# Layer boundaries of a transformer kernel: stage inputs turned and scaled by a product with a diagonal

## The chip, the cores and the metric

The kernel runs on one core of one Trainium2 chip. The metric is the device time in microseconds of one execution. TensorE is PE in the rows (its weight loads PEld), VectorE is DVE, ScalarE is ACT, GpSimd is POOL, and SP is the engine that issues the loads of weights.

## The reference, cut to what matters

256 tokens of 1024 channels pass through latent attention with a convolutional FFN, differential attention with such an FFN, and a hybrid layer (gated delta net, rotary attention, two gates). Each of these five parts has the form below. `g_pre` has one gain per channel, the root one value per token.

```python
def rms_norm(x, g):
    xf = x.astype(jnp.float32)
    y = xf * lax.rsqrt(jnp.mean(xf * xf, -1, keepdims=True) + EPS)
    return (y * g.astype(jnp.float32)).astype(x.dtype)
...
    x = x + rms_norm(part(rms_norm(x, g_pre)), g_post)
```

## The kernel before, in words

The tokens stand on the partitions in `hid` (two token tiles t = 0, 1 of 128 tokens by 1024 channels, f32). The projections need the input turned: `xh` and `xl` hold it with the channels on the partitions, eight blocks b of 128 channels by 256 tokens, as a high part (rounded to the fast f32 format) and the low rest. Every weight chunk is split in the same way (`split_high` L361 on ScalarE, `split_low` L372 on DVE or GpSimd), and `mm3` (L409) makes a product of three fast ones. `project_t` (L421) runs 24 such matmuls over the eight blocks; its argument `arriving` makes the first projection of a stage wait for the low parts of the input as they come.

Between two parts lies a boundary, numbered n for the part that ends (n = 0 latent attention, 1 first FFN, 2 differential attention, 3 second FFN, 4 the end). Every engine has its program written out by hand, and semaphores tie them; an engine's order is the order of the calls.

- The end of the part, `post_*` (L641 to L702). ScalarE squares the accumulators and sums them (`post_square`), DVE multiplies them with the post gain (`post_gained`), adds up the mean, GpSimd raises it to -0.5 (`post_pool`, L674), DVE adds the result to `hid` (`post_add`, L669). `post_dve` (L690) sets DVE's order over tiles and halves (half = 512 channels).
- The input of the next part. ScalarE squares `hid` (`pre_square`, L549), DVE makes the mean (`pre_mean`, L559), GpSimd the root (`pre_pool`, L632). DVE then multiplies each tile and half with root and gain (`pre_norm`, L567, the gain `pre_gain` broadcast over all partitions by DMA), TensorE turns the result (`pre_pe`, L527: first seven filler products L525, then sixteen transpositions L535, then one filler), ScalarE copies the high part (`pre_split_act`, L555) and DVE subtracts (`pre_split_dve`, L627). This serves three boundaries: before the first FFN, before the second FFN, before the delta net. `boundary_pool` (L743) and `start_pool` (L765) load the gains from GpSimd's queue.
- The boundary before differential attention ("the raw boundary", RAW = 2) differs: `raw_pe` (L572) turns `hid` itself, without the root, both token tiles of a block side by side in one bank (`raw_turned`, L584), ScalarE and DVE split with the gain as a per-channel scale (`raw_split_act` L591, `raw_split_dve` L599), and the root enters later through `factor_cols_dve` (L610).

The filler products (`spin`, L522) compute nothing that is used. Behind the splits ScalarE and DVE have weight splits in their queues, then the first convolution of the FFN (L1208, L1252). The delta net begins with the product for its gates (`gates_project_pe`, L1691).

Of the kernel before, what the change touches and what calls it, by code (L numbers as in the profile page):

```python
# [23 lines left out]
P = 128  # L24
TOK = 256
# [84 lines left out]
for _n, _w in (("q_gain", MLA_QB), ("kv_gain", MLA_KVB), ("sub_gain", 1),  # L110
               ("gdn_gain", 1), ("down_gain", KB), ("power", 8), ("conv", HEADS * 12), ("ffn_conv", 2 * FFN_STEPS * 16),
               ("slope", HEADS), ("dt", 2 * HEADS), ("a_log", 2 * HEADS), ("lam", 256), ("diff_gain", KB)):
    _vec(_n, _w)
# [65 lines left out]
def lay_out(a):  # L179
# [34 lines left out]
    pre = np.stack([ng[0, 0], ng[0, 2], ng[1, 0], ng[1, 2], f["pre_norm_w_2"][0]])  # L214
    out["post_gain"] = np.ascontiguousarray(np.broadcast_to(post[:, None], (5, P, D)))
    out["pre_gain"] = np.ascontiguousarray(np.broadcast_to(pre[[1, 3, 4], None], (3, P, D)))
# [53 lines left out]
def build(nc, dram, y_out):  # L270
# [150 lines left out]
    def project_t(pe, out, k, width=P, offset=0, x=None, blocks=KB, arriving=None):  # L421
# [71 lines left out]
    n_ = sems("n", "hid sq mean root hn turned xh xl gain")  # L493
# [94 lines left out]
    def raw_split_act(act, half):  # L588
        act.wait_ge(n_["turned"], 4 * RAW + 2 + half + 1)
        for b in range(4 * half, 4 * half + 4):  # L590
            ins = act.activation(xh[:, b, :], raw_turned(b), ACT.Copy, scale=vcol("diff_gain", b, 1))  # L591
            if b % 2:
                ins.then_inc(n_["xh"], 1)

    def raw_split_dve(dve):
        for b in range(KB):
            if b % 2 == 0:
                dve.wait_ge(n_["xh"], 4 * RAW + b // 2 + 1)
            ins = dve.scalar_tensor_tensor(xl[:, b, :], raw_turned(b), vcol("diff_gain", b, 1), xh[:, b, :], ALU.mult,  # L599
                                           ALU.subtract)  # L600
            if b % 2:
                ins.then_inc(n_["xl"], 1)
# [9 lines left out]
    def factor_pe(pe):  # L612
        pe.wait_ge(n_["hn"], 4 * (RAW - 1) + 2)
# [4 lines left out]
    def factor_dve(dve):  # L618
        dve.wait_ge(n_["hn"], 4 * (RAW - 1) + 3)
        dve.tensor_copy(factor, acc[:, 3, 0:TOK]).then_inc(n_["hn"], 1)  # L620
        dve.wait_ge(n_["hn"], 4 * (RAW - 1) + 4)

    def pre_split_dve(dve, n):
        for half in range(2):
            for t in range(NT):
                dve.wait_ge(n_["xh"], 4 * n + 2 * t + half + 1)
                dve.tensor_tensor(x_part(xl, t, half), turned(t, half), x_part(xh, t, half),  # L627
                                  ALU.subtract).then_inc(n_["xl"], 1)
# [61 lines left out]
    def post_dve(dve, n, p, k):  # L690
# [5 lines left out]
        post_mean(dve, n, 1)  # L696
        post_gained(dve, n, 1, 0, p, k)
        post_add(dve, n, 0, 1)
# [9 lines left out]
    def pre_act_split(act, n):  # L708
        for t in range(NT):
            pre_split_act(act, n, t)  # L710

    def pre_dve(dve, n):
        pre_norm(dve, n, 0, 0)
        pre_mean(dve, n, 1)
        pre_norm(dve, n, 0, 1)
        for half in range(2):
            pre_norm(dve, n, 1, half)
# [6 lines left out]
    def boundary_raw_act(act, n, p, k):  # L724
        post_act(act, n, p, k)
        pre_square(act, RAW, 0)
        for half in range(2):
            raw_split_act(act, half)
        pre_square(act, RAW, 1)

    def boundary_raw_dve(dve, n, p, k):
        post_early_dve(dve, n, p, k)
        raw_split_dve(dve)
# [9 lines left out]
    def boundary_pool(pool, n):  # L743
# [21 lines left out]
    def start_pool(pool):  # L765
# [5 lines left out]
        pool.dma_start(pre_gain[:], dram["pre_gain"][0]).then_inc(n_["gain"], 16)  # L771
# [919 lines left out]
    def gates_project_pe(pe):  # L1691
        chunk_ready(pe, ph["gates"], 4, 0)
        for b in range(KB):
            if b % 4 == 0:
                pe.wait_ge(n_["xl"], 4 * 4 + 2 + b // 2)
            last = mm3(pe, W[2][0:16, 0:TOK], wslot(4, b * 16, (b + 1) * 16), (xh[:, b, :], xl[:, b, :]), b == 0, b == KB - 1)
# [1477 lines left out]
```

## Time and profile before

| | us |
|---|---|
| median of three runs | 1056.98 |
| lowest and highest | 1056.97, 1057.31 |
| the profiled execution, its own time | 1056.94 |
| its span in the profile | 1055.1 |
| TensorE busy in the span | 1026.9 (97%) |
| DVE, ScalarE, GpSimd busy | 667.6, 557.1, 418.1 |

The rows come from the one profiled execution. Times in them are microseconds from the start of the span; 1.8 us of the execution's time lie around it. The idle time of an engine that is not on the chain of waits costs nothing.

### The profile page before, as it was taken

How to read it: one execution, taken by the hardware profiler on the slowest of the kernel's cores; microseconds unless marked ns; L12 is line 12 of the kernel's file. 1: busy time of each engine (PE TensorE's matmuls, PEld its weight loads, DVE VectorE, ACT ScalarE, POOL GpSimd, SP SyncE). 2: the span in 40 equal slices, each digit the busy share in tenths (PEclk: the TensorE clock that was granted, in tenths of full speed). 3: DMA queues.
4: the chain of work that ended last, by engine and by line, in shares of the span. 5: the costliest groups of instructions: out<-in, count | busy, mean ns of one | idle time of the engine just before them, and what ended most of it. 6: DMA issues, size and time to landing. Idle time of an engine off the chain costs nothing.

```text
span 1055.1 us, 21644 instructions
## 1 busy us (share of the span) xinstructions
PE 1026.9 (97%) x8138; PEld 941.0 (89%) x8138; DVE 667.6 (63%) x1094; ACT 557.1 (53%) x1014; POOL 418.1 (40%) x283
## 2 busy tenths in 40 slices
PE   9999999999999999999999999999999999999997
PEld 7788699999978888699999987899999999999996
DVE  4555867767767766777676766766676555554445
ACT  5655665555564654665555556644543455554442
POOL 1000243334333443433343363865653375533331
PEclk9999999999999999999999999999999999999999
DMA  9334456566434443365655624333213245446551
GB/s 354 102 120 140 159 182 206 188 201 191 151 138 160 156 135 128 124 210 184 201 191 167 205 77 160 104 119 120 81 62 121 81 140 157 151 135 215 195 181 42
DMA packets 46284, 161.82 MB, mean 153 GB/s; under 512 B 5264, under 2 KB 6544, under 8 KB 46096
## 3 DMA queue, kind: packets, MB, share of 16 engines
q1 hardware_dynamic: 45072, 156.79, 44.7%
q0 software_dynamic: 1152, 4.19, 1.2%
q8 instruction: 42, 0.69, 0.3%
q14 instruction: 18, 0.15, 0.0%
HBM read 159.91 MB, written 1.05 MB: 153 GB/s over the span
## 4 chain that ended last, share of the span: by engine, by line
PE 89%; DVE 5%; ACT 2%; POOL 2%; issue 1%; DMA 0%; DVEq 0%; SPq 0%; ACTq 0%
PE work L411 13%; PE work L413 13%; PE work L412 13%; PE work L1849 9%; PE acc L411 6%; PE acc L412 6%; PE acc L413 6%; PE work L2567 4%; PE work L2579 3%; PE acc L2579 2%; PE acc L2096 1%; PE acc L2110 1%; PE acc L2112 1%; PE acc L1941 1%; PE work L1387 1%
## 5 line engine op out<-in xcount | busy, mean ns | idle before, releaser
L380 POOL TENSOR_TENSOR low<-raw,high 128x1024 fp32r<-128x1024 f32 x110 | 269.0, 2449 | 276.5 <-ACT high L367 274.0
L380 DVE TENSOR_TENSOR low<-raw,high 128x1024 fp32r<-128x1024 f32 (+1 forms) x185 | 271.0, 1473 | 147.9 <-ACT high L367 147.8
L367 ACT ACTIVATE high<-raw 128x1024 fp32r<-128x1024 f32 (+2 forms) x295 | 298.6, 1026 | 36.6 <-DMA raw<-in_w_out 23.7
L411 PE MATMUL work<-xh,high 128*128 128x256 f32 (+1 forms) x1032 | 290.0, 281 | 2.1 <-DVE v_sb L1534 1.7
L412 PE MATMUL work<-xl,high 128*128 128x256 f32 (+1 forms) x1032 | 287.9, 279 | 0.0
L413 PE MATMUL work<-xh,low 128*128 128x256 f32 (+1 forms) x1032 | 287.8, 279 | 0.0
L411 PEld LDWEIGHTS work<-xh,high 128*128 128x128 f32 (+1 forms) x1032 | 193.2, 187 | 9.0 <-issue 5.6
L412 PEld LDWEIGHTS work<-xl,high 128*128 128x128 f32 (+1 forms) x1032 | 193.3, 187 | 1.7
L413 PEld LDWEIGHTS work<-xh,low 128*128 128x128 f32 (+1 forms) x1032 | 193.3, 187 | 0.2
L1290 POOL TENSOR_TENSOR h<-gelu,cv 128x256 f32<-128x256 f32 x44 | 49.7, 1130 | 194.3 <-ACT gelu L1214 87.6
L1849 PE MATMUL work<-xh,high 128*128 128x256 f32 x256 | 76.7, 300 | 0.0
L1849 PE MATMUL work<-xl,high 128*128 128x256 f32 x256 | 71.6, 280 | 0.0
L1849 PE MATMUL work<-xh,low 128*128 128x256 f32 x256 | 71.4, 279 | 0.0
L412 PE MATMUL acc<-low,hh 128*128 128x512 f32 x164 | 64.3, 392 | 0.0
L411 PE MATMUL acc<-high,hh 128*128 128x512 f32 x164 | 64.2, 391 | 0.0
L413 PE MATMUL acc<-high,hl 128*128 128x512 f32 x164 | 63.8, 389 | 0.0
L1220 ACT ACTIVATE hh<-h 128x256 fp32r<-128x256 f32 x42 | 17.5, 418 | 86.7 <-POOL h L1290 85.7
L1849 PEld LDWEIGHTS work<-xh,high 128*128 128x128 f32 x256 | 48.1, 188 | 2.5
L1849 PEld LDWEIGHTS work<-xl,high 128*128 128x128 f32 x256 | 48.2, 188 | 0.0
L1849 PEld LDWEIGHTS work<-xh,low 128*128 128x128 f32 x256 | 48.1, 188 | 0.0
L1208 ACT ACTIVATE cv<-work,vec 128x256 f32<-128x256 f32 x44 | 24.8, 564 | 40.0 <-PE work L413 40.0
L1293 POOL TENSOR_TENSOR hl<-h,hh 128x256 fp32r<-128x256 f32 x42 | 31.9, 760 | 25.6 <-ACT hh L1220 25.6
(402 smaller groups left out, 2172.5 us busy)
## 6 DMA issues: line engine op xcount, KB each, us to landing
raw<-in_w_ffn SPq DMA_DIRECT2D x130, 512.0 KB, 4.3
raw<-in_w_out SPq DMA_DIRECT2D x39, 512.0 KB, 4.3
raw<-in_w_att SPq DMA_DIRECT2D x32, 512.0 KB, 3.9
raw<-in_w_diff SPq DMA_DIRECT2D x31, 512.0 KB, 3.9
raw<-in_w_gdn SPq DMA_DIRECT2D x24, 512.0 KB, 4.4
raw<-in_w_mla SPq DMA_DIRECT2D x8, 512.0 KB, 3.7
raw<-in_w_gdnz SPq DMA_DIRECT2D x8, 512.0 KB, 4.0
raw<-in_w_mla SPq DMA_DIRECT2D x8, 384.0 KB, 3.3
```

The lines of the kernel that those rows point to most:

```text
L367: act.activation(high[k][:, 0:w], raw[k][:, 0:w], ACT.Copy).then_inc(high_done[k], 1)
L380: eng.tensor_tensor(low[k][:, 0:w], raw[k][:, 0:w], high[k][:, 0:w], ALU.subtract).then_inc(low_done[k], 1)
L411: pe.matmul(out, lhs[0], rhs[0], start=start, stop=False)
L412: pe.matmul(out, lhs[0], rhs[1], start=False, stop=False)
L413: return pe.matmul(out, lhs[1], rhs[0], start=False, stop=stop)
L1208: act.activation((cg, cv)[value][j][:], W[bank][:, 0:TOK], ACT.Identity, scale=ffn_taps(layer, i, j, value, 1, 0), bias=ffn_taps(layer, i, ...
L1220: act.activation(hidden_of(layer, j, i)[0][:], h32[j][:], ACT.Copy).then_inc(f[j]["hh"], 1)
L1290: pool.tensor_tensor(h32[j][:], gelu[j][:], cv[j][:], ALU.mult).then_inc(s["h32"], 1)
L1293: pool.tensor_tensor(low_part[:], h32[j][:], high_part[:], ALU.subtract).then_inc(s["hl"], 1)
L1849: last = pe.matmul(W[x][:, 0:TOK], l[slot][:, b * P:(b + 1) * P], r[:, b, :], start=(s == 0), stop=(s == 23))
L2567: last = pe.matmul(W[0][:, t * TOK:(t + 1) * TOK], x[:, b, t * P:(t + 1) * P], w[k][:, o:o + TOK], start=(b == 0 and term == 0), stop=(b = ...
L2579: last = pe.matmul(out, w[k][:, b * P:(b + 1) * P], x[:, b, :], start=(s == 0), stop=(s == 23))
```

## The change

At the three boundaries the input is turned by a product in full f32 instead of a transposition: the moving operand is no longer the identity but the identity with each token's root on its diagonal, so that the product turns `hid` and scales it at once. DVE makes that diagonal (128x128) in place of the norm of 128x1024 per tile. TensorE goes through the channels by halves and, within a half, through both token tiles, and puts a block's two tiles side by side. ScalarE and DVE split with the gain per channel as at the raw boundary, in blocks of 128x256, eight in place of four of 128x512. The gains of four boundaries stand in the vector table, and the three loads of broadcast gains are dropped. There is one filler fewer in front of the products and none behind. DVE's `post_add` of tile 0, half 1 moves ahead of `post_gained` of tile 1, half 0. The raw boundary keeps its operations and counts block by block. The gates' product goes to another bank. One wait of ScalarE for the constants moves ahead of the first boundary. The diff, cut to its core:

```diff
 def lay_out(a):
-    put("diff_gain", channels(ng[1, 0]))
+    put("pre_gain", np.concatenate([channels(x) for x in (ng[0, 2], ng[1, 0], ng[1, 2], f["pre_norm_w_2"][0])], 1))
...
-    out["pre_gain"] = np.ascontiguousarray(np.broadcast_to(pre[[1, 3, 4], None], (3, P, D)))
 def project_t(...):
-            if arriving == RAW and b % 2 == 0:
-                pe.wait_ge(n_["xl"], 4 * RAW + 1 + b // 2)
-            elif arriving is not None and b % 4 == 0:
-                pe.wait_ge(n_["xl"], 4 * arriving + 2 + b // 2)
+            if arriving is not None and b % 2 == 0:
+                pe.wait_ge(n_["xl"], split_seen(arriving) + b + 2)
...
+    def split_seen(n):
+        return 4 + KB * (n - 1)
+    HN_SEEN = {1: 0, 2: 2, 3: 6, 4: 8}
 def pre_pe(pe, n):
     pe.wait_ge(g["const"], 48)
-        spin(pe, W[3][:], 7)
-        for t in range(NT):
-            for half in range(2):
-                pe.wait_ge(n_["hn"], 4 * (n - 1) + 2 * t + half + 1)
-                for b in range(4):
-                    at = (4 * half + b) * P
-                    last = pe.transpose(work[:, 2 * t + half, b * P:(b + 1) * P], hn[:, t, at:at + P], ident)
+        spin(pe, W[3][:], 6)
+        for half in range(2):
+            for t in range(NT):
+                pe.wait_ge(n_["hn"], HN_SEEN[n] + t + 1)
+                for b in range(4 * half, 4 * half + 4):
+                    last = pe.matmul(raw_turned(b)[:, t * P:(t + 1) * P], hid[:, t, b * P:(b + 1) * P], diag[t],
+                                     start=True, stop=True)
                 last.then_inc(n_["turned"], 1)
-        spin(pe, acc[:, 3, :], 1)
-    def pre_split_act(act, n, t):
-        for half in range(2):
-            act.wait_ge(n_["turned"], 4 * n + 2 * t + half + 1)
-            act.activation(x_part(xh, t, half), turned(t, half), ACT.Copy).then_inc(n_["xh"], 1)
-    def pre_norm(dve, n, t, half):
-        dve.wait_ge(n_["root"], 2 * n + t + 1)
-        if t == 0 and half == 0:
-            dve.wait_ge(n_["gain"], 16 * (n if n < RAW else n - 1))
-        c = cols(half)
-        dve.scalar_tensor_tensor(hn[:, t, c], hid[:, t, c], stat[:, 8 + t:9 + t], pre_gain[:, c], ALU.mult,
-                                 ALU.mult).then_inc(n_["hn"], 1)
+    diag = [hn[:, t, 0:P] for t in range(NT)]
+    def pre_diag(dve, n, t):
+        dve.wait_ge(n_["root"], 2 * n + t + 1)
+        dve.tensor_scalar(diag[t], ident, stat[:, 8 + t:9 + t], None, ALU.mult).then_inc(n_["hn"], 1)
...
-    def raw_split_act(act, half):
-    def raw_split_dve(dve):
+    def turned_gain(n, b):
+        return vcol("pre_gain", KB * (n - 1) + b, 1)
+    def pre_split_act(act, n, half):
+        act.wait_ge(n_["turned"], 4 * n + (2 + half + 1 if n == RAW else 2 * half + 2))
         for b in range(4 * half, 4 * half + 4):
+            act.activation(xh[:, b, :], raw_turned(b), ACT.Copy, scale=turned_gain(n, b)).then_inc(n_["xh"], 1)
+    def pre_split_dve(dve, n):
         for b in range(KB):
             if b % 2 == 0:
+                dve.wait_ge(n_["xh"], split_seen(n) + b + 2)
+            dve.scalar_tensor_tensor(xl[:, b, :], raw_turned(b), turned_gain(n, b), xh[:, b, :], ALU.mult,
+                                     ALU.subtract).then_inc(n_["xl"], 1)
 def post_dve(dve, n, p, k):
         post_mean(dve, n, 1)
+        post_add(dve, n, 0, 1)
         post_gained(dve, n, 1, 0, p, k)
-        post_add(dve, n, 0, 1)
         post_add(dve, n, 1, 0)
 def pre_dve(dve, n):
-        pre_norm(dve, n, 0, 0)
+        pre_diag(dve, n, 0)
         pre_mean(dve, n, 1)
-        pre_norm(dve, n, 0, 1)
-        for half in range(2):
-            pre_norm(dve, n, 1, half)
+        pre_diag(dve, n, 1)
 def boundary_pool(pool, n):
-        if n in (0, RAW):
-            pool.wait_ge(n_["hn"], 4 * n + 4)
-            pool.dma_start(pre_gain[:], dram["pre_gain"][1 if n == 0 else 2]).then_inc(n_["gain"], 16)
 def start_pool(pool):
-        pool.dma_start(pre_gain[:], dram["pre_gain"][0]).then_inc(n_["gain"], 16)
 def gates_project_pe(pe):
-            if b % 4 == 0:
-                pe.wait_ge(n_["xl"], 4 * 4 + 2 + b // 2)
-            last = mm3(pe, W[2][0:16, 0:TOK], ...)
+            if b % 2 == 0:
+                pe.wait_ge(n_["xl"], split_seen(4) + b + 2)
+            last = mm3(pe, acc[0:16, 0, 0:TOK], ...)
```

## Rows read from the trace of the kernel before

**Rows 1.** Page, part 4, the chain of waits: share of the span by engine

```profile
PE 89%; DVE 5%; ACT 2%; POOL 2%; issue 1%; DMA 0%; DVEq 0%; SPq 0%; ACTq 0%
```

**Rows 2.** The chain in order of time, first boundary (start us, us, what)

```profile
119.23 1.00 POOL stat L632
...
122.38 0.86 PE acc L525 x2
```

**Rows 3.** Timeline from 118.9 us (start, us, engine, line, op, out<-in, count, idle before)

```profile
118.94 0.21 DVE L559 TENSOR_SCALAR mean<-stat 128x1 f32<-128x1 f32 x1
...
120.25 1.41 DVE L567 SCALAR_TENSOR_TENSOR hn<-hid,stat,pre_gain_sb 128x512 f32<-128x512 f32 x2 [0.44 <-POOL stat L632]
...
121.06 1.32 PE L535 MATMUL work<-const,hn 128*128 128x128 f32 x8 [0.54 <-DVE hn L567]
...
121.75 1.26 ACT L555 ACTIVATE xh<-work 128x512 fp32r<-128x512 f32 x2 [0.59 <-PE work L535]
...
122.38 1.29 DVE L627 TENSOR_TENSOR xl<-work,xh 128x512 fp32r<-128x512 f32 x2
...
123.22 0.35 PE L411 MATMUL work<-xh,high 128*128 128x256 f32 x1
...
126.10 0.28 PE L411 MATMUL work<-xh,high 128*128 128x256 f32 x1
```

**Rows 4.** Timeline, 112 to 118 us

```profile
112.81 6.17 PE L525 MATMUL work<-const 128*128 128x512 f32 x14
...
114.83 0.68 DVE L656 TENSOR_TENSOR hn<-acc,post_gain_sb 128x512 f32<-128x512 f32 x1
...
115.43 1.41 DVE L669 SCALAR_TENSOR_TENSOR hid<-hn,stat,hid 128x512 f32<-128x512 f32 x2
...
117.25 0.99 POOL L632 TENSOR_TENSOR stat<-mean,vec 128x1 f32<-128x1 f32 x1 [1.70 <-DVE mean L559]
...
117.86 0.63 ACT L549 ACTIVATE hn<-hid 128x512 f32<-128x512 f32 x1 [0.27 <-DVE hid L669]
```

**Rows 5.** Timeline, raw boundary, DVE

```profile
316.40 0.29 DVE L610 TENSOR_SCALAR hn<-const,stat 128x128 f32<-128x128 f32 x1 [0.47 <-POOL stat L632]
```

**Rows 6.** Timeline, raw boundary, from 310.9 us

```profile
310.94 3.03 ACT L591 ACTIVATE xh<-work,vec 128x256 fp32r<-128x256 f32 x8 [1.26 <-PE work L580]
...
311.06 0.55 POOL L632 TENSOR_TENSOR stat<-mean,vec 128x1 f32<-128x1 f32 x1 [1.72 <-DVE mean L559]
...
311.81 3.23 DVE L599 SCALAR_TENSOR_TENSOR xl<-work,vec,xh 128x256 fp32r<-128x256 f32 x8 [0.83 <-ACT xh L591]
...
312.83 0.35 PE L411 MATMUL work<-xh,high 128*128 128x256 f32 x1 [0.41 <-DVE xl L599]
...
315.12 0.36 PE L411 MATMUL work<-xh,high 128*128 128x256 f32 x1
...
315.90 0.28 PE L411 MATMUL work<-xh,high 128*128 128x256 f32 x1
```

**Rows 7.** The chain in order of time, delta net, products in f32

```profile
659.76 3.57 PE acc L1712 x32
```

**Rows 8.** The chain in order of time, raw boundary

```profile
310.94 0.85 ACT xh L591 x2
311.81 0.89 DVE xl L599 x2
```

**Rows 9.** Timeline, start of the first FFN, DVE

```profile
126.96 0.48 DVE L1252 SCALAR_TENSOR_TENSOR cg<-work,vec,cg 128x255 f32<-128x255 f32 x1 [0.42 <-ACT cg L1208]
```

**Rows 10.** Page, part 2 (GB/s by slice) and part 6 (DMA issues)

```profile
GB/s 354 102 120 140 159 182 206 188 201 191 151 138 160 156 135 128 124 210 184 201 191 167 205 77 160 104 119 120 81 62 121 81 140 157 151 135 215 195 181 42
...
pre_gain_sb<-in_pre_gain POOLq DMA_DIRECT2D x3, 512.0 KB, 4.9
```

**Rows 11.** List of waits, the longest for a DMA (us in total, times, longest)

```profile
ACT high L367 <- DMA raw<-in_w_out: 23.7, 6, 4.5
```

**Rows 12.** Busy time by stretch: PE, PEld, DVE, ACT, POOL, granted clock, DMA

```profile
118.00:123.00 5.00, 4.23 (x21) 2.10 (x19) 4.17 (x8) 2.97 (x7) 2.32 (x4) 1.00 0.29 93
```

More of the change, by code:

```diff
@@ L111 @@
                ("gdn_gain", 1), ("down_gain", KB), ("power", 8), ("conv", HEADS * 12), ("ffn_conv", 2 * FFN_STEPS * 16),
-               ("slope", HEADS), ("dt", 2 * HEADS), ("a_log", 2 * HEADS), ("lam", 256), ("diff_gain", KB)):
+               ("slope", HEADS), ("dt", 2 * HEADS), ("a_log", 2 * HEADS), ("lam", 256), ("pre_gain", 4 * KB)):
     _vec(_n, _w)
@@ L210, in lay_out @@
     put("power", np.full((P, 8), -0.5))
-    put("diff_gain", channels(ng[1, 0]))
+    put("pre_gain", np.concatenate([channels(x) for x in (ng[0, 2], ng[1, 0], ng[1, 2], f["pre_norm_w_2"][0])], 1))
     out["vec"] = v
     post = np.stack([ng[0, 1], ng[0, 3], ng[1, 1], ng[1, 3], f["post_norm_w_2"][0]])
-    pre = np.stack([ng[0, 0], ng[0, 2], ng[1, 0], ng[1, 2], f["pre_norm_w_2"][0]])
     out["post_gain"] = np.ascontiguousarray(np.broadcast_to(post[:, None], (5, P, D)))
-    out["pre_gain"] = np.ascontiguousarray(np.broadcast_to(pre[[1, 3, 4], None], (3, P, D)))
     def chunks(name, parts):
@@ L492, in build @@
     g = sems("g", "x second_x const")
-    n_ = sems("n", "hid sq mean root hn turned xh xl gain")
+    n_ = sems("n", "hid sq mean root hn turned xh xl")
     h = sems("h", "qkev s mx sm e p pt ptev vev pv oh ol rope roped turned turned_ev")
@@ L586, in raw_turned @@
         return work[:, b // 2, (b % 2) * TOK:(b % 2) * TOK + TOK]
-    def raw_split_act(act, half):
-        act.wait_ge(n_["turned"], 4 * RAW + 2 + half + 1)
+    def turned_gain(n, b):
+        return vcol("pre_gain", KB * (n - 1) + b, 1)
+    def pre_split_act(act, n, half):
+        act.wait_ge(n_["turned"], 4 * n + (2 + half + 1 if n == RAW else 2 * half + 2))
         for b in range(4 * half, 4 * half + 4):
-            ins = act.activation(xh[:, b, :], raw_turned(b), ACT.Copy, scale=vcol("diff_gain", b, 1))
-            if b % 2:
-                ins.then_inc(n_["xh"], 1)
-    def raw_split_dve(dve):
+            act.activation(xh[:, b, :], raw_turned(b), ACT.Copy, scale=turned_gain(n, b)).then_inc(n_["xh"], 1)
+    def pre_split_dve(dve, n):
         for b in range(KB):
             if b % 2 == 0:
[L598 to L602, printed above, removed]
+                dve.wait_ge(n_["xh"], split_seen(n) + b + 2)
+            dve.scalar_tensor_tensor(xl[:, b, :], raw_turned(b), turned_gain(n, b), xh[:, b, :], ALU.mult,
+                                     ALU.subtract).then_inc(n_["xl"], 1)
     factor_col = [hn[:, t, 0:P] for t in range(NT)]
@@ L612, in factor_pe @@
     def factor_pe(pe):
-        pe.wait_ge(n_["hn"], 4 * (RAW - 1) + 2)
+        pe.wait_ge(n_["hn"], HN_SEEN[RAW] + 2)
         for t in range(NT):
@@ L618, in factor_dve @@
     def factor_dve(dve):
-        dve.wait_ge(n_["hn"], 4 * (RAW - 1) + 3)
+        dve.wait_ge(n_["hn"], HN_SEEN[RAW] + 3)
         dve.tensor_copy(factor, acc[:, 3, 0:TOK]).then_inc(n_["hn"], 1)
-        dve.wait_ge(n_["hn"], 4 * (RAW - 1) + 4)
-    def pre_split_dve(dve, n):
-        for half in range(2):
[L625 to L628, printed above, removed]
+        dve.wait_ge(n_["hn"], HN_SEEN[RAW] + 4)
     def pre_pool(pool, n, t):
@@ L708, in pre_act_split @@
     def pre_act_split(act, n):
-        for t in range(NT):
-            pre_split_act(act, n, t)
+        for half in range(2):
+            pre_split_act(act, n, half)
     def pre_dve(dve, n):
-        pre_norm(dve, n, 0, 0)
+        pre_diag(dve, n, 0)
         pre_mean(dve, n, 1)
-        pre_norm(dve, n, 0, 1)
-        for half in range(2):
-            pre_norm(dve, n, 1, half)
+        pre_diag(dve, n, 1)
     def boundary_act(act, n, p, k):
@@ L726, in boundary_raw_act @@
         pre_square(act, RAW, 0)
-        for half in range(2):
-            raw_split_act(act, half)
+        pre_act_split(act, RAW)
         pre_square(act, RAW, 1)
@@ L732, in boundary_raw_dve @@
         post_early_dve(dve, n, p, k)
-        raw_split_dve(dve)
+        pre_split_dve(dve, RAW)
         diff_setup_dve(dve)
@@ L1693, in gates_project_pe @@
         for b in range(KB):
-            if b % 4 == 0:
-                pe.wait_ge(n_["xl"], 4 * 4 + 2 + b // 2)
-            last = mm3(pe, W[2][0:16, 0:TOK], wslot(4, b * 16, (b + 1) * 16), (xh[:, b, :], xl[:, b, :]), b == 0, b == KB - 1)
+            if b % 2 == 0:
+                pe.wait_ge(n_["xl"], split_seen(4) + b + 2)
+            last = mm3(pe, acc[0:16, 0, 0:TOK], wslot(4, b * 16, (b + 1) * 16), (xh[:, b, :], xl[:, b, :]), b == 0, b == KB - 1)
         last.then_inc(used[4], 1)
@@ L1717, in gates_take_act @@
         act.wait_ge(used[4], ph["gates"].base[4] + 1)
-        act.activation(gates_t, W[2][0:16, 0:TOK], ACT.Copy).then_inc(z_["act"], 1)
+        act.activation(gates_t, acc[0:16, 0, 0:TOK], ACT.Copy).then_inc(z_["act"], 1)
     def gates_beta_act(act):
@@ L3094, in _ @@
         mla_act(act)
+        act.wait_ge(g["const"], 48)
         boundary_act(act, 0, ph["mla"], 2)
@@ L3097, in _ @@
         split_high(act, ph["ffn0"], 4, 0)
-        act.wait_ge(g["const"], 48)
         ffn_act(act, 0)
```

## The prediction, made before the changed kernel was built or run

> **What bounds the kernel now.** I read the chain of waits on the page first: 89% of the end-setting chain is TensorE work [rows 1], so a change pays only where TensorE waits. The chain in order of time shows where that is, in this change's reach: at each of three layer boundaries (start of the first FFN, of the second, of the delta net) it leaves TensorE for the norms. At the first it goes through the second power on GpSimd, 1.00 us, and comes back to TensorE by the filler product L525 at 122.38 [rows 2]. The timeline shows that the filler hides a second path of equal length: the second low part L627 began at 122.38 and took 0.68 us (half the 1.29 for two, plus overlap), so it was there at 123.06; the projection began at 123.22 and its next one at 126.10 [rows 3]. The three boundaries repeat this to within 0.03 us, so I work out one. All are followed by stretches in which TensorE never waits, so what its projection gains or loses arrives at the end.
>
> **The change, part by part** (first boundary; before against after).
>
> Order of the adds. Before, gain (1,0) starts at 114.83 and the two adds at 115.43, 1.41 us for both: 0.75 each, 0.66 from start to start, so the second add starts at 116.09 [rows 4]. After, add (0,1) starts at 114.83, the gain at 115.49, ending 0.68 later at 116.17, and add (1,0) must wait for that: 116.21, taking 0.04 us for the handover. That add is 0.12 us later. But add (1,1) was held by a mean that waited for a square; that square now runs 0.6 us earlier, so mean and add follow at once: 116.87 and 117.00, add done 117.75. Before, it was done 0.03 us ahead of the square at 117.86 [rows 4]: 0.08 us won.
>
> Squares, mean and powers. ScalarE's last square starts 0.03 us after the add, at 117.78; its sum is read at 118.51. The first power took 0.99 us beside a DVE add with two operands in SBUF [rows 4]; the same in place, 117.16 to 118.15. The first diagonal then costs what L610 costs for the same form, 0.28 us [rows 5], and is ready at 118.46, where the norm of one half took 0.75. The mean of the second token tile no longer stands behind that norm: 118.55 instead of 118.94 [rows 3]. Its power starts at 118.83. Here is a choice: beside a norm it took 1.00 [rows 2]; at the raw boundary, with DVE idle, 0.55 [rows 6]. After the change DVE has nothing to do at that moment, so I take 0.55 and keep 0.99 for the range: 119.38. Second diagonal 119.41 to 119.69, against a norm that started at 120.25.
>
> Six fillers instead of seven: 12 instructions at 0.43 from 112.81 [rows 4] end near 118.1, before the first diagonal, so they delay nothing; seven would have ended at 119.0 and delayed the first products by half a microsecond, though not the second tile's.
>
> The products. A 128x128 product in full f32 is two instructions here, a transposition one. Thirty-two such instructions at L1712 took 3.57 us, 0.11 each [rows 7], so a product costs 0.22 and a group of four 0.89 us. First half of the channels: tile 0 runs at 118.5 to 119.4 in the wait; tile 1 starts at 119.75 (0.06 after the diagonal, as L535 after its norm [rows 3]) and its last result is there at 120.84. ScalarE may then split both tiles side by side: 120.88, against 121.75 for the corresponding block before [rows 3]. That is 0.87 us won.
>
> A rule could speak against this. The Trainium skill, "FP8 and Floating Point Precision", section TensorE Precision Notes, counts true FP32 as four passes through the array; read as four transpositions a product would cost 0.45, and the sum would come out near +8 us instead of about nothing. Rival C works that case out from rows.
>
> The evacuation. Before, one plain split of 128x512 (1.26 us for two) and one subtraction followed. After, the raw boundary is the pattern, same operations, same shapes, same buffers: ScalarE start 310.94, TensorE 312.83, so 1.89 us [rows 6], two splits 0.85 and two low parts 0.89 of it [rows 8]. TensorE would start at 120.88 + 1.89 = 122.77 instead of 123.22: 0.45 us earlier.
>
> What is late next. The low parts come at 0.39 us each (3.23 for eight, 0.89 for two [rows 6, 8]), TensorE eats a block in 0.35, so it stutters: at the raw boundary it started block 6 at 315.12 and the next projection at 315.90, 3.07 us after its start [rows 6]; before, here, the same stretch takes 2.88 [rows 3]. That gives back 0.19. And here, unlike there, the second half's sixteen instructions run after the first half's: their last starts at 122.35, is done at 122.62, and ScalarE's fifth split waits until 122.66 where its own pace (0.36 each) allowed 122.32. Sixth split done 123.51, fifth low part 123.54 instead of 123.33: 0.21 us more. Next projection: 122.77 + 3.07 + 0.21 = 126.05 against 126.10. **0.05 us per boundary**, 0.15 for three. With the second half's delay gone it would be 0.26; with the power at 0.99, a loss of 0.39.
>
> Behind it. ScalarE ends its splits at about 124.2 (before 123.0) and DVE at 125.2 (before 124.3), so the weight splits queued behind them are a microsecond late, and the first tap, which before started at 126.96 after a 0.42 us wait [rows 9], comes near 127.5. No product needs it before the second step, about 8 us on. Zero, at most 0.1 per FFN. At the delta net both engines wait for the gates' product anyway.
>
> Removed transfers. Three of 512 KB leave GpSimd's queue [rows 10], with about 0.5 us of issue each. Behind the first stands a power that waits for DVE long after, behind the second the first FFN's product that waits for a gelu, behind the third a weight split, which then starts a microsecond earlier for a product that TensorE reaches only after three projections (8 us). In the first slice 354 GB/s flow [rows 10], so the first is worth 1.5 us of transfer there; yet the longest wait for a transfer is of the last stage [rows 11], and none follows that load. Zero; 1.5 is its bound. The 24 more columns of the vector table, the earlier wait of ScalarE for constants long loaded, and the raw boundary's single-step counts: zero, since nothing in it moves.
>
> The end of the kernel. The last boundary has the new order too, and there add (1,0) feeds add (1,1) with no mean between: the 0.12 us stay. Loss 0.12.
>
> Sum: -0.15 + 0.12 = -0.03 us on the profiled execution's 1056.94, which is the median of 1056.98 to 0.04. **1057.0.** A measurement can tell about 0.2%, 2.1 us, from no change.
>
> **The rivals.**
> A. The gain comes whole (faster). If the transfer at the start did delay weights, 1.5 us return; if the second half doesn't hold up ScalarE, 3 x 0.26 more: -2.3 + 0.12 gives 1054.8. For it: transfers fill the first slice. Against: no wait on them behind that load. It needs both. 0.07.
> B. The power stays at 0.99 because its cost isn't the neighbour on DVE: 3 x 0.39 + 0.12 = +1.3, 1058.2. The two prices at the same line speak against it. 0.07; still within 0.2%.
> C. The products cost more (slower). It decides between the second diagonal and ScalarE's fifth split, where twelve products lie in a row: above 0.23 us a product the boundary loses, above 0.29 measurably. At 0.45, twice the 0.22 taken, the second half is 12 x 0.22 = 2.7 us later: +2.65 a boundary, 1065.0. For it: no row shows this very pair of operands. Against: L1712 and its 0.11. 0.03. (Four transpositions of 0.11 would be this case, as the page named above can be read.)
> D. The clock falls (slower). Granted 1.00 in the stretch with the norms [rows 12]; the change takes out one filler in front and one behind, and leaves pauses of 0.4 us. If it halved (2.4 to 1.2 GHz), the 2.7 us of products in that row and the 2.8 of the projection double: about 5.4 us a boundary, 1073. 0.03.
> E. The change doesn't do what it says: the two tiles of a block aren't ready side by side any earlier than before, because something not seen holds the second tile, and the projection starts at 123.22 as before. Then the stutter is all that is left: 3 x 0.40 + 0.12 = +1.3, 1058.2. 0.02.
>
> **How the numbers follow.** The forecast has 0.78. Its own range, by the ends above, is 1056.3 (3 x -0.26 and the 0.12) to 1058.2 (B). Faster is A, 0.07; slower C and D, 0.06; the rest same, 0.87. The range reaches a little toward A, 1055.6 to 1058.5 with the 0.1 per FFN, and leaves out A, C and D.
>
> **What would show it.** In the changed profile: L632's second power at 0.55; 32 instructions of products per boundary at 0.11 each; ScalarE's split starting 0.9 us earlier, with a pause before its fifth; TensorE's projection starting 0.4 us earlier with short waits at blocks 2, 4 and 6; GpSimd's reload lines gone; PEclk 1.00. The forecast is wrong if the projection's second one starts more than 0.5 us from 126.05, or if the difference lies outside the three boundaries.

## The result, and where the profile after puts the time

The changed kernel took 1073.44 us (median of 4 runs, 1073.13 to 1073.63), the kernel before 1057.14 beside it: ratio 1.0151, 95% interval 1.0138 to 1.0164. The forecast was 1057.0 and its range ended at 1058.5. The profiled execution took 1073.13 us, its span was 1071.3 us against 1055.1.

The page of the kernel after, parts 1 and 2 (busy us, share, instructions; GB/s in 40 slices), part 4 (chain of waits by engine) and part 6 (DMA issues):

```profile
PE 1041.1 (97%) x8174; PEld 957.1 (89%) x8174; DVE 665.1 (62%) x1100; ACT 561.0 (52%) x1026; POOL 416.5 (39%) x280
...
GB/s 332 101 118 135 140 194 206 189 174 196 151 125 167 149 140 115 137 156 181 196 182 189 191 87 145 112 119 113 86 61 120 80 139 156 154 140 198 195 177 40
...
PE 89%; DVE 5%; ACT 2%; issue 1%; POOL 1%; DMA 0%; DVEq 0%; SPq 0%; ACTq 0%
...
post_gain_sb<-in_post_gain POOLq DMA_DIRECT2D x5, 512.0 KB, 4.0
```

The shares of the chain are those of [rows 1] to a per cent, and the loads of the broadcast gains are gone from part 6 [rows 10]. Yet TensorE's busy time is 1041.1 us; on the page before it was 1026.9. So some 14 of the 16 us are time in which TensorE works, not time in which it waits.

**The first boundary did what was predicted.** Timeline of the kernel after (start, us, engine, line, op, out<-in, count, idle before):

```profile
113.29 5.31 PE L521 MATMUL work<-const 128*128 128x512 f32 x12
...
118.66 0.29 DVE L563 TENSOR_SCALAR hn<-const,stat 128x128 f32<-128x128 f32 x1 [0.44 <-POOL stat L619]
...
119.29 0.55 POOL L619 TENSOR_TENSOR stat<-mean,vec 128x1 f32<-128x1 f32 x1 [0.67 <-DVE mean L556]
...
119.88 0.29 DVE L563 TENSOR_SCALAR hn<-const,stat 128x128 f32<-128x128 f32 x1 [0.66 <-POOL stat L619]
...
121.42 1.57 ACT L589 ACTIVATE xh<-work,vec 128x256 fp32r<-128x256 f32 x4 [2.45 <-PE work L537]
...
123.20 1.57 ACT L589 ACTIVATE xh<-work,vec 128x256 fp32r<-128x256 f32 x4 [0.22 <-PE work L537]
...
123.31 0.36 PE L409 MATMUL work<-xh,high 128*128 128x256 f32 x1
...
126.61 0.28 PE L409 MATMUL work<-xh,high 128*128 128x256 f32 x1
```

The fillers start 0.48 us later than before (113.29, 112.81 in [rows 4]); take that off each of the times here. ScalarE's start is then 120.94 (forecast 120.88), its fifth split 122.72 (122.66), TensorE's projection 122.83 (122.77), the next one 126.13 (126.05; before 126.10 [rows 3]). The second power took 0.55.

**The second boundary didn't.** GpSimd and DVE there, kernel after:

```profile
447.60 0.55 POOL L619 TENSOR_TENSOR stat<-mean,vec 128x1 f32<-128x1 f32 x1 [0.67 <-DVE mean L556]
448.10 0.60 POOL L733 DMA_DIRECT2D post_gain_sb<-in_post_gain  x1
448.72 2.35 POOL L378 TENSOR_TENSOR low<-raw,high 128x1024 fp32r<-128x1024 f32 x1
```

```profile
446.96 0.29 DVE L563 TENSOR_SCALAR hn<-const,stat 128x128 f32<-128x128 f32 x1 [0.44 <-POOL stat L619]
...
448.19 2.98 DVE L563 TENSOR_SCALAR hn<-const,stat 128x128 f32<-128x128 f32 x1 [0.66 <-POOL stat L619]
```

The same in the kernel before, GpSimd:

```profile
444.36 0.60 POOL L749 DMA_DIRECT2D post_gain_sb<-in_post_gain  x1
446.16 0.54 POOL L752 DMA_DIRECT2D pre_gain_sb<-in_pre_gain  x1 [1.20 <-DVE hn L567]
446.71 2.41 POOL L380 TENSOR_TENSOR low<-raw,high 128x1024 fp32r<-128x1024 f32 x1
```

Before, the load of the gains waited for DVE's norm, and the weight split L380 stood behind it. With the load gone the split comes at once, and the second diagonal takes 2.98 us where every other took 0.29: it ends (451.17) with the split (451.07). In the kernel before, VectorE had other work beside the split (446.71 to 449.12):

```profile
445.77 2.68 DVE L627 TENSOR_TENSOR xl<-work,xh 128x512 fp32r<-128x512 f32 x4
448.38 2.97 DVE L380 TENSOR_TENSOR low<-raw,high 128x1024 fp32r<-128x1024 f32 x2
```

Its four subtractions, one operand of each in PSUM (`work`), kept their 0.68 us each, as at the other boundaries; its two weight splits, both operands in SBUF, took 2.97 us, where two with GpSimd idle take 2.36 (a4, below). So the split doesn't hold everything on VectorE. Two readings of TensorE in the kernel after follow, its timeline and the busy time by stretch (stretch and its length, busy us of PE, PEld, DVE, ACT and POOL, granted clock, DMA share and GB/s):

```profile
451.22 4.57 PE L537 MATMUL work<-hn,hid 128*128 128x128 f32 x24 [2.75 <-DVE hn L563]
455.55 0.36 PE L409 MATMUL work<-xh,high 128*128 128x256 f32 x1
```

```profile
450.00:451.00 1.00, 0.00 (x0) 0.00 (x0) 1.00 (x1) 0.00 (x0) 1.00 (x1) 1.00 0.91 356
451.00:452.00 1.00, 0.78 (x5) 0.79 (x6) 0.16 (x1) 0.00 (x0) 0.07 (x1) 0.78 0.15 57
452.00:453.00 1.00, 1.00 (x6) 1.00 (x6) 0.00 (x0) 0.00 (x0) 0.00 (x0) 0.50 0.82 233
...
455.00:456.00 1.00, 1.00 (x11) 1.00 (x11) 0.58 (x2) 0.17 (x1) 0.00 (x0) 1.00 0.00 0
```

TensorE idles 2.75 us; then the granted clock goes from 1.00 to 0.50 (of the two levels 2.4 and 1.2 GHz the lower) until 455, and 24 instructions take 4.57 us.

From the first filler to the start of the second projection this boundary takes 17.62 us, in the kernel before 13.28.

**The rest is everywhere.** Groups of TensorE by form, kernel after (busy us, mean ns of one):

```profile
L409 PE MATMUL work<-xh,high 128*128 128x256 f32 x1024 | 291.7, 285 | 2.7 <-DVE v_sb L1514 1.7 <-DVE xl L595 0.8
L411 PE MATMUL work<-xh,low 128*128 128x256 f32 x1024 | 289.2, 282 | 0.0
L410 PE MATMUL work<-xl,high 128*128 128x256 f32 x1024 | 288.1, 281 | 0.0
...
L409 PE MATMUL acc<-high,hh 128*128 128x512 f32 x164 | 64.8, 395 | 0.0
L411 PE MATMUL acc<-high,hl 128*128 128x512 f32 x164 | 64.7, 395 | 0.0
L410 PE MATMUL acc<-low,hh 128*128 128x512 f32 x164 | 64.2, 392 | 0.0
```

The same groups before:

```profile
L411 PE MATMUL work<-xh,high 128*128 128x256 f32 x1024 | 287.7, 281 | 2.1 <-DVE v_sb L1534 1.7 <-DVE xl L599 0.4
L412 PE MATMUL work<-xl,high 128*128 128x256 f32 x1024 | 285.7, 279 | 0.0
L413 PE MATMUL work<-xh,low 128*128 128x256 f32 x1024 | 285.6, 279 | 0.0
...
L412 PE MATMUL acc<-low,hh 128*128 128x512 f32 x164 | 64.3, 392 | 0.0
L411 PE MATMUL acc<-high,hh 128*128 128x512 f32 x164 | 64.2, 391 | 0.0
L413 PE MATMUL acc<-high,hl 128*128 128x512 f32 x164 | 63.8, 389 | 0.0
```

The same instructions in the same number, five of the six groups 2 to 6 ns longer and one (`low`, `hh`) unchanged. These durations overlap, since a product of 256 columns is recorded for some 280 ns and the next one starts after 117, so their sums are no times. From start to start, the means of the first three groups go from 117.1, 116.7 and 117.1 ns (`xh,high`, `xh,low`, `xl,high`) to 119.9, 119.0 and 118.3; with the products of the delta net the three have some 4000 instructions, so by an estimate that is 8 us. By the starts of the fillers and of the projection, the kernel after is behind by 0.48 us at the first boundary (113.29 to 112.81), by 4.61 at the second (441.62 to 437.01), by 8.14 at its projection (455.55 to 447.41), by 12.58 at the third (643.68 to 631.10) and by 16.17 at the last product (1063.64 to 1047.47). Some 3.5 us come in the second boundary up to its projection, 4.3 with what is late behind it; the rest, 12 us, grows in the stretches between, where no instruction of the change stands.

What differs in those stretches is the place of the tensors. The 24 new columns make the vector table 96 bytes longer in each partition, and every SBUF tensor allocated behind it moves by 96. The weight buffers `high0` to `high4` and `low0` to `low4` stand ahead of the table and stay, at multiples of 4096 bytes from the first buffer. By the sizes in the kernel (an estimate that takes each as rounded up to 32 bytes), `xh` and `xl` move from 32 to 128 bytes behind such a multiple, counted modulo 256, and the FFN's `hh` and `hl` from 0 to 96. The weight buffers of the sixth slot (`high5`, `low5`) stand behind the table too and move with the rest.

### The profile page after: what moved, and what is told of

The parts are those of the page before. It is cut to its first block, busy times and chain, and to the rows that moved or that the text cites. A ratio compares the mean times of both kernels' runs of the same rounds, so it can differ in the third digit from the quotient of the medians.

```text
span 1071.3 us, 21728 instructions
## 1 busy us (share of the span) xinstructions
PE 1041.1 (97%) x8174; PEld 957.1 (89%) x8174; DVE 665.1 (62%) x1100; ACT 561.0 (52%) x1026; POOL 416.5 (39%) x280
## 4 chain that ended last, share of the span: by engine, by line
PE 89%; DVE 5%; ACT 2%; issue 1%; POOL 1%; DMA 0%; DVEq 0%; SPq 0%; ACTq 0%
PE work L409 13%; PE work L411 13%; PE work L410 13%; PE work L1829 9%; PE acc L409 6%; PE acc L411 6%; PE acc L410 6%; PE work L2547 4%; PE work L2559 3%; PE acc L2559 2%; PE acc L2076 1%; PE acc L2090 1%; DVE hid L656 1%; PE acc L2092 1%; PE work L537 1%
## 5 line engine op out<-in xcount | busy, mean ns | idle before, releaser
L409 PE MATMUL work<-xh,high 128*128 128x256 f32 x1024 | 291.7, 285 | 2.7 <-DVE v_sb L1514 1.7
L411 PE MATMUL work<-xh,low 128*128 128x256 f32 x1024 | 289.2, 282 | 0.0
L410 PE MATMUL work<-xl,high 128*128 128x256 f32 x1024 | 288.1, 281 | 0.0
L409 PEld LDWEIGHTS work<-xh,high 128*128 128x128 f32 x1024 | 193.1, 189 | 7.7 <-issue 3.6
L410 PEld LDWEIGHTS work<-xl,high 128*128 128x128 f32 x1024 | 193.4, 189 | 1.7
L411 PEld LDWEIGHTS work<-xh,low 128*128 128x128 f32 x1024 | 192.7, 188 | 0.0
L1829 PE MATMUL work<-xh,high 128*128 128x256 f32 x256 | 77.0, 301 | 0.0
L1829 PE MATMUL work<-xl,high 128*128 128x256 f32 x256 | 72.0, 281 | 0.0
L1829 PE MATMUL work<-xh,low 128*128 128x256 f32 x256 | 71.8, 280 | 0.0
L1829 PEld LDWEIGHTS work<-xh,high 128*128 128x128 f32 x256 | 48.2, 188 | 2.5
L1829 PEld LDWEIGHTS work<-xl,high 128*128 128x128 f32 x256 | 48.3, 189 | 0.0
L1829 PEld LDWEIGHTS work<-xh,low 128*128 128x128 f32 x256 | 48.2, 188 | 0.0
```

Of the source, the lines that this page charges most:

```text
L409: pe.matmul(out, lhs[0], rhs[0], start=start, stop=False)
L410: pe.matmul(out, lhs[0], rhs[1], start=False, stop=False)
L411: return pe.matmul(out, lhs[1], rhs[0], start=False, stop=stop)
L1829: last = pe.matmul(W[x][:, 0:TOK], l[slot][:, b * P:(b + 1) * P], r[:, b, :], start=(s == 0), stop=(s == 23))
```

## The experiments

Two theories. **Placement**: the products' step depends on where their tensors lie, 11 to 12 us. **Held diagonal**: the split takes something from VectorE, 4 to 5 us with what follows. Rivals: the new products and splits cost it themselves; the clock alone.

**a1, the kernel before with the table longer**

```diff
-("lam", 256), ("diff_gain", KB)
+("lam", 256), ("diff_gain", KB), ("unused", 24)
```

> The kernel before, with 24 unused columns at the end of the vector table: no instruction differs, every tensor in SBUF behind the table lies 96 bytes further on, as in the kernel after. Theory 'placement' (the step of the long products depends on where their operands lie): the steps grow as in the kernel after, 117 to 121 ns in the FFN's first products, 227 to 234 in its second ones, 117 to 122 in the last stage, and the time is 11 to 12 us over the kernel before, 1068 to 1069. Theory 'the new products and splits' (the change's own work costs the 16 us): no difference, 1057.0 within 0.5. If the 96 bytes matter only together with the change's instructions, also 1057.

1069.80 us, ratio 1.0118 (1.0101 to 1.0135), 0.8 over its range: 12.4 us for 96 unused bytes, none of the change in it. Its groups:

```profile
L411 PE MATMUL work<-xh,high 128*128 128x256 f32 x1024 | 291.9, 285 | 2.1 <-DVE v_sb L1534 1.7 <-DVE xl L599 0.4
L413 PE MATMUL work<-xh,low 128*128 128x256 f32 x1024 | 289.5, 283 | 0.0
L412 PE MATMUL work<-xl,high 128*128 128x256 f32 x1024 | 288.4, 282 | 0.0
```

285, 283, 282 ns, as after to 1 ns. From start to start the three are at 119.9, 119.0 and 118.2 ns, and the growth of all of TensorE's steps, added up, comes to some 12 us. Placement stands.

**a2, the kernel after moved back to the same place modulo 256**

```diff
     vec = sb("vec", [P, NVEC])
+    pad(160)
```

> The kernel after with 160 unused bytes behind the vector table, so that all that follows lies 256 bytes further on than in the kernel before, and so at the same place within 256 bytes. Theory 'placement': the long products return to 117 and 227 ns, and what is left is the second boundary's loss of 4 to 5 us: 1061 to 1062.5. Theory 'the new products and splits': still 1073.4.

1062.45 us, ratio 1.0043 (1.0026 to 1.0060): 11.0 us of the 16.3 go. Its executions lie further apart than others (1061.39 to 1064.04).

**a3, GpSimd waits for the second diagonal; a4, both repairs**

```diff
 def boundary_pool(pool, n):
+    if n == RAW:
+        pool.wait_ge(n_["hn"], HN_SEEN[3] + 2)
     pool.wait_ge(q_["upd"], 4 * n + 4)
     pool.dma_start(post_gain[:], dram["post_gain"][n + 1])
```

> The kernel after, with one wait at the second boundary alone: GpSimd starts its reload and the weight split behind it only when the second diagonal is done. Theory 'VectorE held by GpSimd' (the diagonal took 2.98 us instead of 0.29 beside that split): the diagonal takes 0.3 again, TensorE's pause of 2.75 us goes, and with it the stretch at half clock; 4 to 5 us less than the kernel after, 1068.5 to 1069.5. Rival 'the clock alone' (the clock falls there for want of the removed filler, whatever the diagonal does): the pause goes, the half clock stays, at most 2.5 us less. Rival 'something else held the diagonal': no difference, 1073.4.

> Both repairs in one kernel: the 160 bytes and the wait of GpSimd. If placement and the held diagonal are all of the difference, 1056.8 to 1057.5, which is what the prediction said of the change itself; if the two theories leave something out, the rest of the 16.3 us shows here.

a3: 1069.24 us, 4.2 less than the kernel after. a4: 1057.49 us, ratio 1.0000 (0.9990 to 1.0009), with the granted clock at 1.00 through the second boundary in both. The two repairs together return all of the loss; the change with both is the change that was forecast. VectorE in a4, second boundary:

```profile
443.89 0.29 DVE L564 TENSOR_SCALAR hn<-const,stat 128x128 f32<-128x128 f32 x1 [0.66 <-POOL stat L620]
...
449.76 2.36 DVE L379 TENSOR_TENSOR low<-raw,high 128x1024 fp32r<-128x1024 f32 x2
```

**What holds the diagonal: b4 and c1** (both with the 160 bytes). b4 leaves GpSimd alone and gives the second boundary's diagonals to ScalarE; c1 puts a3's wait behind the reload's issue, ahead of the split.

```diff
+    act.activation(diag[t], ident, ACT.Copy, scale=stat[:, 8 + t:9 + t]).then_inc(n_["hn"], 1)
```

> The kernel after with the 160 bytes, GpSimd not waiting, and the two diagonals of the second boundary made by ScalarE instead of VectorE. Theory 'VectorE is held by GpSimd's split' (the two share something that ScalarE doesn't): ScalarE makes the second diagonal in 0.2 to 0.4 us beside the same split, no pause of 2.75 us, no half clock, 1057 to 1058. Rival 'the memory's rows are held' (the diagonal's place in SBUF is busy whichever engine writes it) or 'the power's result comes late': the pause stays, 1061.5 to 1063, as with the bytes alone (1062.5).

> The kernel after with the 160 bytes, and GpSimd's wait for the second diagonal put behind the issue of its reload instead of ahead of it: the issue (0.60 us, it began 0.09 us before the held diagonal) runs beside the diagonal, only the weight split waits. 'The split holds VectorE': the diagonal takes 0.3 us, 1057 to 1058. 'The issue of the reload holds it': about 3 us for the diagonal, 1062, as without the wait.

b4: 1057.62 us (0.9996 to 1.0015). The split is recorded in the same place, 0.53 us behind the start of the second diagonal (in the kernel after 448.72 to 448.19), and ScalarE's diagonal took 0.40:

```profile
443.95 0.40 ACT L713 ACTIVATE hn<-const,stat 128x128 f32<-128x128 f32 x1 [0.62 <-POOL stat L620]
```

```profile
443.86 0.60 POOL L740 DMA_DIRECT2D post_gain_sb<-in_post_gain  x1
444.48 2.37 POOL L379 TENSOR_TENSOR low<-raw,high 128x1024 fp32r<-128x1024 f32 x1
```

c1: 1057.19 us (0.9987 to 1.0006); GpSimd and VectorE:

```profile
444.00 0.60 POOL L734 DMA_DIRECT2D post_gain_sb<-in_post_gain  x1
444.62 2.37 POOL L379 TENSOR_TENSOR low<-raw,high 128x1024 fp32r<-128x1024 f32 x1
```

```profile
444.09 0.29 DVE L564 TENSOR_SCALAR hn<-const,stat 128x128 f32<-128x128 f32 x1 [0.66 <-POOL stat L620]
```

So it is the split, not the issue, and VectorE, not the tensor's place. The wait costs nothing that shows: the split is recorded 0.62 us behind the issue's start with it and without it.

**How the 5 us divide: c2 and d2** (160 bytes, GpSimd not waiting). Fillers between the first and the second tile's products keep TensorE busy while the diagonal is late: six in c2, as here, and three in d2.

```diff
     for t in range(NT):
+        if n == 3 and half == 0 and t == 1:
+            spin(pe, W[3][:], 6)
```

> The kernel after with the 160 bytes, GpSimd not waiting, and six more filler products (6 x 0.43 = 2.6 us) between the first and the second tile's products at the second boundary: TensorE is busy in the pause, the diagonal stays late. If the loss of 5 us (1062.5 against 1057.5) is the pause of 2.7 us and, as its follower, a granted clock of 0.50 for some 5 us: the clock stays at 1.00 and the time is 2.5 to 3 us over the repaired kernel, 1060 to 1060.7. If the clock falls for another reason: 1062.5 as before.

> As the run with the filled pause, with three fillers instead of six. Six are twelve instructions and took 5.32 us, so that the products of the second tile started 2.2 us behind the diagonal; three take 2.6 us, which is the pause. 'Pause and clock': the clock stays at 1.00, the second tile's products start when the late diagonal is there, 2.7 us late, and nothing more is lost: 1059.4 to 1060.4, between the 1057.5 without the pause and the 1062.5 with pause and half clock. If the clock falls all the same: 1062 to 1063.

c2: 1061.64 us, over its range, by a slip of mine: six fillers are twelve instructions and ran 5.32 us, so the fillers themselves held the products. d2 took 1060.55 us (ratio 1.0019 to 1.0041), 0.15 over its range. TensorE in d2:

```profile
444.59 2.74 PE L522 MATMUL work<-const 128*128 128x512 f32 x6
447.51 2.94 PE L540 MATMUL work<-hn,hid 128*128 128x128 f32 x24 [0.18 <-DVE hn L566]
```

The diagonal still took 2.98 us, the clock stayed at 1.00, and the 24 instructions took 2.94 us instead of 4.57. In a2, the same program without these fillers, the profiled execution (the slowest of its four) shows

```profile
448.33 5.49 PE L538 MATMUL work<-hn,hid 128*128 128x128 f32 x24 [2.75 <-DVE hn L564]
```

Against a4 (1057.49) the late diagonal costs 3.1 us by the medians, and the clock behind the pause another 1.9 (d2 to a2), where the intervals of the two ratios overlap. The traces divide it without that doubt: from the first filler to the start of the second projection a4 takes 13.31 us, d2 16.00, the kernel after 17.62 and a2 18.57. So the late diagonal costs 2.7, and the clock 1.6 to 2.6, by the execution. The clock falls because of the pause, not for want of the filler that was removed: a3 and a4 have no more fillers than the kernel after, no pause, and a clock of 1.00.

**The rule of placement: b1, b2, d3, a1.** The kernel before with 32, 64, 128 (and 96) unused bytes behind the table.

> The kernel before with 32 unused bytes behind the vector table. The step of 96 bytes that cost 12.4 us moved the products' operands from a multiple of 64 bytes plus 32 to a multiple of 64 and the other way round; 32 bytes do the same. Theory 'the place within 64 bytes decides': slow as with 96, 1068 to 1070. Theory 'the place within 256 bytes decides': anything between 1057 and 1070, other than with 96. Theory 'each move by chance': no relation.

> The kernel before with 64 unused bytes behind the vector table. 'The place within 64 bytes decides': every operand keeps its place within 64 bytes, so 1057 within 1, products at 117 and 227 ns. 'The place within 128 or 256 bytes decides': steps over 117 in a part of the products, 1060 to 1070.

> The kernel before with 128 unused bytes behind the vector table. 'The place within 128 bytes decides': 1057 within 1, steps of 117 and 227 ns. 'The place within 256 bytes, or still more, decides': steps over 117 ns in the first products, 1060 to 1072.

| bytes | us | ratio to before (95%) | TensorE busy, us |
|---|---|---|---|
| 0 | 1057.2 | 1 | 1026.9 |
| 32 | 1056.12 | 0.9991 (0.9982 to 1.0001) | 1025.8 |
| 64 | 1071.97 | 1.0140 (1.0123 to 1.0157) | 1042.8 |
| 96 | 1069.80 | 1.0118 (1.0101 to 1.0135) | 1039.7 |
| 128 | 1065.75 | 1.0076 (1.0060 to 1.0091) | 1035.9 |

Places modulo 64 would have made 64 free and 32 and 96 alike, and places modulo 128 would have made 128 free: both fell. With 256 bytes (a4, another program) nothing is lost. Time and TensorE's busy time move together to within 1.2 us.

**Place or distance: d4.** The 96 bytes stand ahead of the first weight buffer, so that all of the kernel's tensors move together.

```diff
+    pad(96)
     raw = [sb(f"raw{k}", [P, 1024]) for k in range(5)]
```

> The kernel before with 96 unused bytes in front of its first buffer, so that the weight buffers, constants and tables move by 96 bytes together with all that lies behind them. The move of the tensors behind the vector table alone cost 12.4 us. 'The distance between the operands of a product decides' (modulo 256): all distances are as in the kernel before, 1057 within 1. 'The place itself decides': slow, 1065 to 1075.

1057.13 us, ratio 0.9998 (0.9989 to 1.0007), TensorE busy 1027.2 us. The same 96 bytes cost 12.4 us between the weights and the inputs, and nothing ahead of both. In this move it is how the tensors lie to one another that counts, not where they lie.

**One operand alone: b3.** 96 bytes ahead of `hh` and `hl`, in the kernel before. What is allocated behind them up to the delta net moves too, but none of the operands of the first products.

> The kernel before with 96 unused bytes in front of the buffers of the FFN's activated channels only: the stationary operand of the FFN's second products (and what the attention layers keep behind it) moves, the moving operand of its first products and both weight buffers don't. If it is each product's own operand that decides: the second products (three groups of 164 in the rows) go from 227 to 230 and 234 ns, which is 2 to 3 us, 1059 to 1060, and the first products stay at 117. If one misplaced tensor slows every product: 1065 or more. If the stationary operand's place doesn't matter: 1057.

1060.18 us, ratio 1.0028 (1.0018 to 1.0038), 0.2 over its range. The first products keep 281, 279, 279 ns; the second products have

```profile
L411 PE MATMUL acc<-high,hh 128*128 128x512 f32 x164 | 64.8, 395 | 0.0
L413 PE MATMUL acc<-high,hl 128*128 128x512 f32 x164 | 64.8, 395 | 0.0
L412 PE MATMUL acc<-low,hh 128*128 128x512 f32 x164 | 64.8, 395 | 0.0
```

against 391, 389 and 392. So the loss sits in the products whose operand moved.

**A placement better than both: c3, c4, d1.** 32 bytes (b1) had helped the first products (280, 278, 278 ns) and hurt the second (393, 393, 395). c3 moves `xh` and `xl` by 32 and everything behind by 256, in the kernel before; c4 is the same in the kernel after, with a3's wait; d1 moves all behind the table of the kernel after by 288, with c1's wait. The diff is that of c3; c4 has 192 for the 32, and d1 has 192 and no second pad.

```diff
     vec = sb("vec", [P, NVEC])
+    pad(32)
...
     xl = sb("xl", [P, KB, TOK], F32R)
+    pad(224)
```

> The kernel before with 32 unused bytes behind the vector table and 224 behind the low inputs: the normed inputs lie 32 bytes further within 256 bytes (which made their products' step 116.0 to 117.9 instead of 116.8 to 118.7 ns, and 114 instead of 118 in the delta net's), the FFN's second products' and the last stage's operands where they were (where 32 bytes had cost 227 to 233 ns). If each operand's place counts by itself, the gains add up without the losses: 2 to 4 us less than before, 1053.3 to 1055.3. If not: 1056 to 1057.

> The kernel after with the same placement as the run of the kernel before with 32 and 224 bytes, and with GpSimd's wait for the second diagonal. If placement and the change's mechanism are independent, it equals that run within 0.5 us (the change itself is worth nothing that can be measured), 1053.5 to 1055.5, and is faster than both kernels.

> The kernel after with 192 unused bytes behind the vector table (everything behind it 288 bytes further on than in the kernel before, which is 32 within 256) and GpSimd's wait between its reload and the weight split. The kernel before with all moved by 32 bytes took 1056.1. If placement within 256 bytes and the change are independent: 1055.8 to 1056.8. If not (the kernel after lost 1.4 us more than the kernel before in the last pair of equal placement): 1057 to 1058.

All three missed: 1057.65 (ratio 0.9991 to 1.0009), 1059.01 (1.0002 to 1.0020), 1057.33 (0.9988 to 1.0006). The second products in c3:

```profile
L413 PE MATMUL acc<-high,hh 128*128 128x512 f32 x164 | 64.8, 395 | 0.0
L415 PE MATMUL acc<-high,hl 128*128 128x512 f32 x164 | 64.2, 391 | 0.0
L414 PE MATMUL acc<-low,hh 128*128 128x512 f32 x164 | 63.7, 389 | 0.0
```

Here `high`, `low`, `hh` and `hl` lie byte for byte where they lie in a4, where the three took 392, 389 and 392 ns. Only `xh`, `xl` and what stands around them lie 32 bytes elsewhere. c4 repeats the three values (395, 391, 389), so they are no scatter. Nor did the first products gain in c3 what they had in b1: 281, 279, 279 ns. So "each product by its own operands", which b3 suggested, isn't the whole rule.

Two pairs also leave an end open. c4 took 1.4 us more than c3 beside it (TensorE busy 1029.5 to 1028.1), and d1 1.2 more than b1, from another batch, though each pair has the same placement modulo 256, where a4 and the kernel before differ by 0.1. No run says why. No version beat the kernel before by more than its interval.

## Why the prediction was wrong

- **The boundary's own mechanism: right.** Order of the adds, powers, diagonals, products, split, stutter: at the first boundary every start named here, from the first diagonal on (118.18 by this count, forecast 118.46 less its 0.28), came within 0.08 us of the forecast. The boundary gave +0.03 us instead of -0.05; in a4 the three gave +0.05, +0.03 and 0.00, each after a projection that started 0.35 to 0.38 earlier. The products were a little under-priced: 24 instructions took 2.94 us in d2, 0.245 a product for the 0.22 in the sum. The whole, with the two causes below taken out, is a4 at 1057.49 for a forecast of 1057.0.
- **"The 24 more columns of the vector table ... zero": wrong, 11 to 12.4 us.** I priced the columns as a transfer and not as a shift of all that is allocated behind them. What the step should have asked is which tensors a longer one pushes. In the runs, 96 bytes alone took the kernel before from 1057.35 to 1069.80. Nothing in the rows would have given the price; the kernel's own four odd pads (32, 224, 192, 224 bytes) could have been a hint that placement matters here.
- **"Removed transfers ... behind the third a weight split, which then starts a microsecond earlier ... Zero": wrong, 4.2 to 5.0 us** (a3 under after; a4 under a2). I asked who needs the split's result and not beside whom it would now run. The runs showed a diagonal of 2.98 us in place of 0.29. The removed wait had kept the split behind VectorE's last norm, and so beside subtractions that it doesn't hold. I also called the split's boundary one of three alike; in this it was the only one: at the third, GpSimd has no split there, and the diagonal took 0.29.
- The same rows held a warning: a power took 0.99 us beside a VectorE instruction with two operands in SBUF and 0.55 beside none [rows 4, 6]. I used it to price the power, in the one direction, and didn't turn it round. The Trainium skill, "SBUF — State Buffer", section SBUF: two separate sides, says it both ways: GpSimd shares a pair of ports with VectorE's instructions in a fast two-port mode or with two inputs in SBUF, and the one that starts first has it for its whole length. The trace agrees in the length, 2.98 us for a diagonal of 0.29, its end 0.10 behind the split's, and in the subtractions with an operand in PSUM, which weren't held. It doesn't agree in the order of the recorded starts, the diagonal's 0.53 us ahead of the split's, and no row shows the mode in which the diagonal ran.
- **Rivals.** A: no, the first slice moved 332 GB/s for 354 and nothing came back. B: no, the power took 0.55. C: no, the products took 0.245 us each at a clock of 1.00, not 0.45. D named 1073 and the right number for the wrong reason: the clock fell at one boundary and not at three, for about 3.4 us, behind a pause that D didn't have; it is worth 1.6 to 2.6 us. E: no, TensorE's projection started 0.39 earlier (122.83 for 123.22).
- **The wording "the difference lies outside the three boundaries"**, given as a sign that would refute the forecast, is what the trace showed for some 12 us. No rival named placement or the split.

## What to carry to other kernels

Before pricing an edit that lengthens or drops a buffer, list which tensors it moves, and in the trace after it compare the mean time of the untouched matmuls first: if they all changed, pad the placement back (modulo 256 bytes served here) before judging the edit. Before removing a wait, ask what stands behind it on its engine and what will now run beside it; Here a GpSimd split with both operands in SBUF held a VectorE instruction that works in SBUF alone, and left those with an operand in PSUM as they were. An idle TensorE of some 2.7 us cost up to as much again in clock.

## What the runs showed of the hardware that I had not expected

- Placement alone, with the same instructions: 1056.1 to 1072.0 us, 1.5%, in 1 to 6 ns from the start of one matmul to the next (for `xh,high` 116.4 ns with 32 bytes, 117.1 with none, 120.5 with 64). Distances between tensors decide, as far as one move of all together shows, which was free (1057.13). The rule is open: modulo 64 and 128 are excluded, 256 fits what ran, own operands alone don't explain c3, and whether the other engines' accesses take part wasn't tried.
- A 128x128 `tensor_scalar` on VectorE was held to the end of a GpSimd instruction that the profile has starting 0.53 us after it (448.72 to 448.19). With a wait that makes the split truly later, its recorded start is still 0.62 behind the issue. The recorded start of a GpSimd instruction behind a DMA issue doesn't tell when it takes hold; why is open.
- ScalarE made the same diagonal in 0.40 us, at the same distance from the same split. By the records it ended 0.13 us ahead of the split's start, but so would VectorE's 0.29 us have.
- VectorE's subtractions with one operand in PSUM took 0.68 us each beside GpSimd's split, as without it.
- After the same pause of 2.75 us the granted clock stayed at 0.50 for some 3.4 us in one execution (kernel after) and for some 7 us in another (a2, from before 448 until past 454).
